# A layer kernel whose indexer runs earlier, whose decay comes from tanh, and whose first head pair is prepared in the dense stage

## What is computed

```
xn = rmsnorm(x);  p = xn @ w_in          # 3072 columns: r k v wd ad | g | q_down kv_down k_idx w_idx | g_attn
# recurrent branch, 8 heads of 64
xs = p_shift + (prev - p_shift) * mu     # r, k, v, wd, ad
wlog = -softplus(-(w0 + tanh(wd) @ w_up)) - 0.5
decay = exp(-exp(wlog));  a = sigmoid(a0 + ad @ a_up)
kk = k*k_k / max(|k*k_k|, 1e-12);  k = k * (1 + (a-1)*k_a)
S = S*decay + (S @ -kk) (kk*a)' + v k';  y = S @ r        # step by step over the tokens
y = groupnorm(y) + sum(r*k*r_k) * v;  y * silu(g)
# attention branch, 8 heads
score = sum_h w_idx_h * relu(q_idx_h . layernorm(k_idx))  # causal, the 128 best keys of each token
o = softmax(q_abs . c_kv over these keys) @ c_kv @ w_uv;  o * silu(g_attn)
x = rmsnorm(x + concat(y, o) @ w_out)
```

## Time and profile before

| | |
|---|---|
| median of 3 runs | 1549.8 us (1547.76 to 1549.83) |
| profiled execution | 1560.24 us, its span 1558.5 us |
| PE busy | 1478.3 us, 95% of the span |
| DVE, ACT, POOL busy | 1002.0, 507.5, 486.1 us |
| mean granted clock of PE | 0.961 of full |
| chain that ended last | PE 88%, DVE 8%, ACT 2%, issue 1% |

### The profile page before, as it was taken

The page is one execution under the profiler, slowest core; times in us unless marked ns, Lnnn a source line. Parts: engine busy times, 40 slices in busy tenths (PEclk is TensorE's granted clock), DMA queues, the critical chain, the costliest instruction groups (busy, mean ns, idle before and its releaser), DMA issues.

```text
span 1558.5 us, 18633 instructions
## 1 busy us (share of the span) xinstructions
PE 1478.3 (95%) x7530; PEld 1181.7 (76%) x7530; DVE 1002.0 (64%) x1395; ACT 507.5 (33%) x684; POOL 486.1 (31%) x131
## 2 busy tenths in 40 slices
PE   7999888689989899999999999989999999999997
PEld 6778555377678888788888887768877888888886
DVE  4669976843584545766996995473246888885122
ACT  5442366343333332312222222422133333332211
POOL 0004020001253432243434444234442344443440
PEclk9999979789899899999999999999998999999998
DMA  6322000020132322123233332222231333323221
GB/s 179 110 80 81 1 1 1 1 83 28 55 122 95 110 81 81 54 81 108 82 108 92 98 108 82 81 81 82 94 96 54 109 87 102 103 87 101 90 79 54
DMA packets 165798, 125.60 MB, mean 81 GB/s; under 512 B 9195, under 2 KB 163602, under 8 KB 165714
## 3 DMA queue, kind: packets, MB, share of 16 engines
q1 hardware_dynamic: 163506, 122.19, 25.8%
q10 hardware_dynamic: 2208, 2.23, 0.4%
HBM read 122.31 MB, written 2.10 MB: 80 GB/s over the span
## 4 chain that ended last, share of the span: by engine, by line
PE 88%; DVE 8%; ACT 2%; issue 1%; DMA 0%; SPq 0%; DVEq 0%; ACTq 0%
PE bank L414 24%; PE bank L415 24%; PE bank L416 24%; PE bank L366 2%; PE bank L581 1%; PE bank L946 1%; PE bank L962 1%; PE bank L396 1%; PE bank L814 1%; PE bank L540 1%; DVE m_blk L1937 1%; DVE tmp L1935 1%; DVE op_lo L1691 1%; PE bank L813 1%; DVE rs_gn L2071 1%
## 5 line engine op out<-in xcount | busy, mean ns | idle before, releaser
L1149 POOL TENSOR_TENSOR w_lo<-w_raw,w_hi 128x2048 fp32r<-128x2048 f32 (+1 forms) x102 | 467.5, 4583 | 828.3 <-ACT w_hi L1196 800.8
L414 PE MATMUL bank<-op_hi,w_hi 128*128 128x512 f32 x1384 | 548.7, 396 | 18.0 <-DVE op_lo L1670 6.1
L415 PE MATMUL bank<-op_lo,w_hi 128*128 128x512 f32 x1384 | 543.7, 393 | 0.0
L416 PE MATMUL bank<-op_hi,w_lo 128*128 128x512 f32 x1384 | 543.5, 393 | 0.0
L414 PEld LDWEIGHTS bank<-op_hi,w_hi 128*128 128x128 f32 x1384 | 262.1, 189 | 78.6 <-issue 12.6
L416 PEld LDWEIGHTS bank<-op_hi,w_lo 128*128 128x128 f32 x1384 | 262.0, 189 | 56.5
L415 PEld LDWEIGHTS bank<-op_lo,w_hi 128*128 128x128 f32 x1384 | 262.2, 189 | 56.2 <-issue 1.2
L1196 ACT ACTIVATE w_hi<-w_raw 128x2048 fp32r<-128x2048 f32 (+1 forms) x110 | 208.5, 1895 | 293.5 <-PE bank L416 289.3
L2188 DVE SCALAR_TENSOR_TENSOR bank<-pad_b,par,bank 128x512 f32<-128x512 f32 x232 | 175.3, 756 | 7.8
L2355 DVE TENSOR_TENSOR tmp<-tmp,conv_f 128x512 f32<-128x512 f32 x22 | 101.5, 4616 | 16.1 <-ACT tmp L1617 16.1
L2096 DVE TENSOR_TENSOR x_res<-bank,x_res 128x512 f32<-128x512 f32 x16 | 11.0, 690 | 103.0 <-PE bank L416 102.9
(11 more groups left out here) (377 smaller groups left out, 1805.8 us busy)
## 6 DMA issues: line engine op xcount, KB each, us to landing
w_raw<-in_w_in SPq DMA_DIRECT2D x30, 1024.0 KB, 5.1
w_raw<-in_w_up SPq DMA_DIRECT2D x44, 512.0 KB, 5.1
w_raw<-in_w_in SPq DMA_DIRECT2D x35, 512.0 KB, 5.1
w_raw<-in_w_kv SPq DMA_DIRECT2D x8, 1024.0 KB, 5.9
w_raw<-in_w_down SPq DMA_DIRECT2D x8, 1024.0 KB, 5.0
w_raw<-in_w_out SPq DMA_DIRECT2D x4, 1024.0 KB, 5.0
w_raw<-in_w_att_out SPq DMA_DIRECT2D x4, 1024.0 KB, 5.0
w_raw<-in_w_a_out SPq DMA_DIRECT2D x4, 1024.0 KB, 5.0
```

The source lines that it names most:

```text
L414: nc.tensor.matmul(b[:, 0:width], h, xh[:, x0 + k, 0:width], start=start and k == ks[0], stop=False)
L415: nc.tensor.matmul(b[:, 0:width], h, xl(x0 + k, width), start=False, stop=False)
L416: mm = nc.tensor.matmul(b[:, 0:width], l, xh[:, x0 + k, 0:width], start=False, stop=stop and k == ks[-1])
L1149: nc.gpsimd.tensor_tensor(w_lo[u % 2][:, 0:nk, :], w_raw[u % 2][:, 0:nk, :], w_hi[u % 2][:, 0:nk, :].bitcast(F32), ALU.subtract).then_inc( ...
```

## The change

**Indexer.** PE does the query norm before wa, the variance of the index keys between the two tiles of r (a new argument `between`), the index queries behind r, the logits of query tile 1 between the tiles of k, those of tile 2 behind k and of tile 3 behind v. DVE and ACT follow: scores of tiles 1 to 3 are added by the unit v, and the rounds begin behind k. The sigmoids of the gates get buffers of their own (`sig_t`).

**Key norms.** All four pairs' squares go to a buffer `kk_sq` while the keys arrive; 16 products, one square root and one reciprocal behind the unit g of half 1 take the place of four such steps in the head stage. The result is `kk_tok`, 32 columns.

**Tanh.** Sigmoid(z) is written as (1 + tanh(z/2))/2. The 1 goes into the scan's second operation, the halves into scales and constants; Exp and Tanh then follow each other without a table load.

**First pair.** z, a and the spread norms of pair 0 stand between the two ga units, its bonus product behind them, and DVE does key_terms(0) before the last two gate products. In the head loop all is one pair ahead: pair 1 and strict_upper(0) in attention_start, pair h+2 in round h, strict_upper(h+1) ahead of the transposes.

**Substitution.** Its 31 steps go over heads 3 to 6, as 8, 7, 7 and 9. POOL's memset of `inv` moves from pair 0 to behind the last pair.

**Loads.** SP also waits for the product mT of half 1.

```
@@ PE
-            unit_tiles("wa", 0, oh, ol, tiles=1)
-            pe.wait_ge(sem("sq_q"), 2)
+            pe.wait_ge(sem("sq_q"), 2)
...
+            unit_tiles("wa", 0, oh, ol, tiles=1)
...
+            unit_tiles("r", 0, oh, ol, between=index_variance)
+            index_queries()
+            unit_tiles("k", 0, oh, ol, between=lambda: index_logits(1))
+            index_logits(2)
             unit_tiles("v", 0, oh, ol)
+            index_logits(3)
...
+            b = bank("kk")
+            pe.wait_ge(sem("kk_sq"), NI)
+            for i in range(NI):
+                for c in range(NT):
+                    n = 2 * NT * i + 2 * c
+                    mm = nc.tensor.matmul(b[:, n:n + 2], kk_sq[:, i, c * P:c * P + P], pair_ones[:, 0:P:HD], start=True, stop=True)
+            done(mm, "kk")
...
+            unit_tiles("ga", 0, oh, ol)
+            decay_and_rate(0)
+            norms_spread(0)
+            unit_tiles("ga", 1, oh, ol)
+            key_bonus(0)
...
             for h in range(NH):
                 if h + 1 < NH:
                     scores(h + 1)
                 if h + 2 < NH:
                     absorbed_query(h + 2)
                 if h + 1 < NI:
-                    decay_and_rate(h + 1)
-                    key_norms(h + 1)
+                    strict_upper(h + 1)
+                if h + 2 < NI:
+                    decay_and_rate(h + 2)
+                    norms_spread(h + 2)
                 probabilities_turned(h)
...
                 latent_out(h)
-                if h < NI:
-                    strict_upper(h)
-                if h + 1 < NI:
-                    key_bonus(h + 1)
+                if h + 2 < NI:
+                    key_bonus(h + 2)
@@ SP
             evacuated(sp, ("o", NI - 1))
+            filled(sp, ("mT", 1))
@@ ACT
-                evac(A(prep[0][:, 0:T], take(act, ("z", i))[:, :], ACT.Sigmoid, bias=pcol("w0", i)), ("z", i))
+                evac(A(prep[0][:, 0:T], take(act, ("z", i))[:, :], ACT.Tanh, scale=0.5, bias=half_wa[:, i:i + 1]), ("z", i))
...
-                A(tmp[0][:, 0:516], prep[2][:, 0:516], ACT.Exp, scale=-KAPPA).then_inc(sem("exps"), 1)
+                A(tmp[0][:, 0:516], prep[2][:, 0:516], ACT.Exp, scale=-0.5 * KAPPA).then_inc(sem("exps"), 1)
@@ DVE
+                    elif (half, w) == (0, 1):
+                        index_scores(2)
+                        topk_rounds(2)
+                    elif (half, w) == (0, 2):
+                        index_scores(3)
+                        topk_rounds(6)
+                    else:
+                        topk_rounds((22, 30, 37)[w])
...
+                topk_rounds((13, 43)[half])
...
+                if half == 0:
+                    topk_rounds(48)
...
+                    key_terms(0)
...
-                    substitution(10 * (h - NI), 10 * (h - NI) + 10 + (h == NH - 2))
+                    substitution(steps_at[h - 1], steps_at[h])
```

More of the change, by code:

```diff
@@ L271, in build @@
         both_g = misc[:, 107:115]
-        kk_tok = misc[:, 99:107]
+        half_wa = misc[:, 115:123]
+        half_ka = misc[:, 123:127]
         dec = misc[:, 65:81]
@@ L421, in plain, with unit_tiles @@
                 return lambda k, width: t[:, k, 0:width]
-            def unit_tiles(what, i, xh, xl, width=T, tiles=2, ready=None, branch=None, order=range(CH)):
+            def unit_tiles(what, i, xh, xl, width=T, tiles=2, ready=None, branch=None, order=range(CH), between=None):
                 u = next_unit(what)
```

327 lines of the change are left out of this document (162 added, 165 removed).

## The result

The changed kernel took 1541.7 us, the median of 20 executions (1526.9 to 1549.0); the kernel before, in 20 executions beside it, 1553.8 us (1547.8 to 1563.0). The medians are 12.1 us apart; the ratio, 0.990 with a 95% interval of 0.988 to 0.992, makes it 15.4. The profiled execution took 1539.8 us, 20.4 less than that of before.

What follows compares the result with a forecast made beforehand. PE was taken to bound the dense stage, a PE-ACT-DVE chain the heads, DVE the substitution. Terms -23.2, +4.2 and -6.5 gave -25.5 us, from a median of 1549.8 to 1524 us; range 1513 to 1537.

Steps and rivals of the forecast that it cites:

- To u_blk: Dense and head stages: the transposition of u_blk starts at 239.1 instead of 262.27, -23.2 us.
- the query products: End of the dense stage: pair 0's four query products end at 190.4 instead of 181.5, +8.9 us.
- the low price: Dense stage: sixteen new norm products of two columns cost 4.1 us, bounds 0 and 7.4.
- The memset: Head stage: the moved memset of inv meets DVE's scaling of the probabilities, 2.5 to 3.3 us lost.
- The substitution: Behind u_blk: DVE-bound, one more head adds 4.23 us; last transposition ends at 287.0, -19.0 us.
- The hold: Side blocks: loads held until mT no longer delay PE's instructions; -6.5 us, bounds 0 and -7.7.
- Rival A: Side blocks: PE's hole stays or only moves; -19 us, 1531 us; chance 0.20.
- Behind the first chunk: From PE's first product with the state onward: gains carry over one to one, nothing lost.
- B: Head loop: PE runs at 1.2 GHz through more of it, 10 us lost, 1534 us; chance 0.13.
- D: Dense stage: weight halves of units 7 and 8 late in DVE's queue, up to 32 us lost, 1556; chance 0.04.
- E: Head stage: ACT's own chain replaces PE's wait, three times 5.25 us of gain lost, 1540; chance 0.03.
- C: Head stage and last head: clock holds, pair 0's wait is shorter, -7 us, 1517 us; chance 0.10.

Runs made afterwards that it cites:

- again: The changed kernel unaltered, run and profiled a second time; 1540.9 us, median of 6.
- memset_early: The changed kernel with POOL's memset of inv moved to pair 0, behind the gate products; 1528.1 us, median of 5, ratio 0.985.
- after: The changed kernel unaltered: its first profile, 1539.8 us; in means, its three profiles together.
- before: The kernel without the change, unaltered: first profile 1560.2 us; in means, its four profiles together.
- no_hold: The changed kernel without SP's new wait for mT ahead of the loads; 1541.3 us, median of 6, ratio 0.992.
- three moves: The changed kernel with memset of inv in pair 0, bonus product behind first query product, index keys' mean ahead of DVE's shift and split; 1529.4 us, median of 12.

## Why the prediction was wrong

**To u_blk, right.** Forecast -23.2, measured -22.8 in the mean. The dense stage's end (177.0, measured 176.9), the wait at the variance product (2.5, 2.46), the last mask (174.1, 173.1) and the head (14.6, 14.18) came out of the rows; the query products, forecast 8.9 us later, end 6.4 later in the first profile and 10.3 in again. The mean is right partly by luck, since two errors cancel: the first profile, with a nearly full clock, has the transposition 3 us sooner than forecast, and the lower clock behind the variance wait and behind the norm products, up to 5 us in time (again), was not in the sum; I had taken the low price for these products because the clock ahead of them was full, and not asked what it is behind them.

**The memset, mechanism right, size too small.** Forecast "2.5 to 3.3 lost"; it was 3.5 up to u_blk (memset_early), and 1.5 to 1.9 behind it, since PE had gone down to the lower level while it waited. The Trainium skill (SBUF — State Buffer, SBUF: two separate sides) has DVE, in some of its modes, and GpSimd hold a shared pair of ports exclusively, the other blocked for the whole instruction. The trace agrees: the scaling, begun at 228.20 under POOL's product of 227.50, ends 0.08 us behind the memset that follows that product, so POOL's second instruction came ahead of it too.

**The substitution, step mis-sized.** The term is the one more head, 4.23 us: from u_blk to the last transposition it is 50.2 us in the mean of the three profiles of after and 43.8 in before, so 6.5. Without the memset's clock (memset_early) it is 48.5, that is 4.7. The step failed by leaving out the clock at which PE meets the stage: the rows of one more head were priced for DVE alone, while DVE waited 1.67 us for the gate product at 239.76.

**The hold, step wrong.** Forecast -6.5, measured -4.2 in the mean, -3.3 and -3.7 where it alone was changed. The step "PE's instructions stand behind the 3 MB" is right for 3.4 us of the hole, since the packet of instructions starts that much later; its reason, that the stop "ends as the transfers end", is not, for the packet lands 1.5 us before they do (321.7, 323.2). The remaining 1.4 to 2.1 us are there with no load under way, and with them the clock at 0.50 behind: the 2.9 us of clock, which I took to go with the hole, stayed for the most part. The rule of the Trainium skill (Runtime: NRT & Kernel Launch, Instruction fetch mechanics), by which fetching is hidden by the pace of issue and the hold gives nothing, does not agree with the runs either: no_hold has 4.79 us of hole, the changed kernel 1.41, each ending 1.4 to 1.5 us behind the landing of PE's packet. Rival A, "the hole stays or only moves", had half of it right.

**Behind the first chunk, term put at nothing.** The changes were to "carry over one to one", but 3.9 us were lost there in the mean, by the clock: from the first chunk to the end the three profiles of the changed kernel have 63 us at 0.50 and the four of before 54, which is 4.5 us in time. In the first 60 us of that it is 14.8 against 3.4. The profile of before had 13.7 us at 0.50 in the scan, which three further profiles of it had not.

**The base.** The sum was made against a profile of 1560.2 and then lowered by 10.4, its distance to the median of 3 executions. Over 20 the median is 1553.8; the distance is 6.4. That alone puts the forecast 4.0 us too low, a quarter of the miss of 17.7. The stages above make 8.7, and the remaining 5 are nearly all which executions happened to be profiled: the three of the changed kernel average 1537.5 where its median is 1541.7, the four of before 1554.3 where theirs is 1553.8. A spread of 2 us in three executions was taken for the spread of the kernel; it is 15 us.

**Rivals.** B, "the clock", gave 1534 and named the head loop. The loop itself runs faster than forecast (0.96); the clock was lost before it, behind the memset, and in the scan. D did not occur: PE waits for no weight half between 60 and 176. E did not: the head lasts 14.2. C, the clock holding through the head stage and a shorter wait for pair 0, is what the first profile shows up to u_blk (0.96, 2.59 us, the transposition 3.1 us ahead of the forecast), and not behind it.

## What to carry to other kernels

A wait or a row of tiny products on PE costs its own time and then, at half the clock, part of what follows; price a new one with the stretch behind it, by the dearer of the rows, and look for another place in the order before accepting it: three moves, with no work taken away, gained another 11 us together, though the medians do not tell what the two beside the memset's add. A memset, or any long instruction of POOL, belongs where DVE waits for something else. Before a profile is used as the base of a sum, it should be laid beside several others of the same kernel, stage by stage, since the difference between two profiles of one kernel was as large here as two thirds of the whole gain.

## What the runs showed of the hardware

PE has a hole of 1.4 to 2.1 us in the run of 32x32 products with no load beside it, and of 4.8 to 5.1 us with 3 MB of loads under way. Both end 1.3 to 1.6 us behind the landing of a 16 KB packet of PE's instructions, and with the loads the packet starts some 3.3 us later against the moment at which PE stops. A DVE scaling of 0.29 us takes 4.46 when POOL's memset of 4096 columns runs, and ends 0.08 behind it. The clock falls in the scan, 10 or 21 us in, for 14 to 27 us or not at all, while PE is busy 38.75 of 40 us; what decides it is not shown. The times of the changed kernel follow the mean clock: 1526.9 us at 0.978, 1549.0 at 0.962.
